# Cached attention of the sample tokens: from one stage after the attention groups to one step inside each of the four groups

## The reference, cut to what matters

```
def cached_attention(q, k_new, v_new, k_past, v_past, sinks, table):
    k_all = jnp.concatenate([k_past, k_new], axis=1)
    v_all = jnp.concatenate([v_past, v_new], axis=1)
    ...
    valid = (dist >= 0) & (dist < WINDOW)
    return sink_attend(q, k_all, v_all, dist, valid[None, None], sinks, table)

y = o.reshape(B, T, ATT_WIDTH) * jax.nn.silu(gate)
return x + rmsnorm(y @ w_out, g_post)
```

## Time and profile before

| | us |
|---|---|
| median of the runs shown | 3196.15 (3192.51 to 3197.89) |
| the profiled execution | 3192.12 |
| its span, first to last instruction | 3190.2 |
| PE busy | 2826.0 (89%) |
| DVE, ACT, POOL busy | 1177.4, 712.4, 1342.1 |
| mean granted TensorE clock | 0.941 |

### The profile page before, as it was taken

The page is one execution under the profiler, slowest core; times in us unless marked ns, Lnnn a source line. Parts: engine busy times, 40 slices in busy tenths (PEclk is TensorE's granted clock), DMA queues, the critical chain, the costliest instruction groups (busy, mean ns, idle before and its releaser), DMA issues.

```text
span 3190.2 us, 50357 instructions
## 1 busy us (share of the span) xinstructions
PE 2826.0 (89%) x17686; PEld 2725.6 (85%) x17686; DVE 1177.4 (37%) x2805; ACT 712.4 (22%) x1671; POOL 1342.1 (42%) x2013
## 2 busy tenths in 40 slices
PE   3999999999979999589999999999999802699994
PEld 3999999999979999488899889988988802699993
DVE  8344355433550000655541553455155401100006
ACT  4023212221140101223221322233133201110103
POOL 1244354443533333774556455554645400133323
PEclk7999999999989999899999999999999955799996
DMA  8221121211132222721111111111211111322227
GB/s 247 81 67 59 43 63 59 63 43 59 56 133 73 66 75 67 293 92 38 51 47 52 47 44 58 46 44 41 65 38 50 42 52 43 124 69 70 73 101 244
DMA packets 302784, 245.38 MB, mean 77 GB/s; under 512 B 11978, under 2 KB 279466, under 8 KB 301515
## 3 DMA queue, kind: packets, MB, share of 16 engines
q1 hardware_dynamic: 250684, 180.38, 17.9%
q10 hardware_dynamic: 51944, 63.03, 5.7%
HBM read 184.54 MB, written 63.15 MB: 78 GB/s over the span
## 4 chain that ended last, share of the span: by engine, by line
PE 81%; DVE 8%; SPq 6%; issue 2%; ACT 1%; DMA 1%; DVEq 0%; POOL 0%; ACTq 0%; POOLq 0%
PE ps L498 71%; SPq L355 6%; PE ps L535 3%; PE ps L590 2%; PE ps L616 2%; PE ps L603 2%; DVE xsp L1042 1%; DVE xsp L1244 1%; ACT pt L926 1%; DVE xsp L1107 1%; DVE xsp L1038 1%; DVE rstd L1215 1%; DMA vc<-out_sample_v 0%; PE ps L637 0%; PE ps L706 0%
## 5 line engine op out<-in xcount | busy, mean ns | idle before, releaser
L498 PE MATMUL ps<-xsp,wsp 128*128 128x344 f32 x14976 | 2422.9, 322 | 86.8 <-DVE mx L1264 24.3
L498 PEld LDWEIGHTS ps<-xsp,wsp 128*128 128x128 f32 x14976 | 2367.2, 189 | 130.4 <-issue 63.4
L397 POOL CAST wsp<-raw 128x512 fp32r<-128x512 f32 x272 | 219.1, 806 | 1178.9 <-PE ps L498 1048.1
L402 POOL TENSOR_SCALAR raw<-raw,prm 128x128 f32<-128x128 f32 x640 | 242.5, 396 | 475.7 <-PE ps L498 475.7
L399 POOL TENSOR_TENSOR wsp<-raw,wsp 128x512 fp32r<-128x512 f32 x272 | 400.0, 1470 | 50.4 <-POOL wsp L397 50.4
L1202 DVE TENSOR_TENSOR acc<-acc,stg 128x1032 f32<-128x1032 f32 x32 | 39.5, 1236 | 666.7 <-ACT stg L848 666.7
L409 POOL TENSOR_TENSOR wsp<-raw,wsp 128x512 fp32r<-128x512 f32 x160 | 220.5, 1378 | 29.4 <-POOL wsp L406 29.4
L406 POOL TENSOR_SCALAR wsp<-raw 128x128 fp32r<-128x128 f32 x640 | 184.1, 314 | 32.4 <-POOL raw L402 32.4
L847 ACT ACTIVATE stg<-ps 128x344 f32<-128x344 f32 x96 | 45.4, 473 | 641.3 <-PE ps L498 641.3
L913 ACT ACTIVATE mx<-mx 128x2 f32<-128x2 f32 x128 | 26.3, 206 | 442.6 <-DVE mx L1270 442.6
L916 ACT ACTIVATE pp<-pp,mx 128x256 f32<-128x256 f32 (+1 forms) x256 | 123.5, 484 | 0.0
(11 more groups left out here) (193 smaller groups left out, 2064.0 us busy)
## 6 DMA issues: line engine op xcount, KB each, us to landing
raw<-in_a_w_in SPq DMA_DIRECT2D x128, 256.0 KB, 2.8
raw<-in_b_w_qg SPq DMA_DIRECT2D x128, 256.0 KB, 2.8
o_t<-stg ACTq DMA_DIRECT2D x32, 516.0 KB, 3.6
xsp<-o_t SPq DMA_DIRECT2D x8, 2064.0 KB, 12.9
raw<-in_a_w_out SPq DMA_DIRECT2D x64, 256.0 KB, 2.7
raw<-in_b_w_out SPq DMA_DIRECT2D x64, 256.0 KB, 2.7
xsp<-x_t SPq DMA_DIRECT2D x7, 2064.0 KB, 17.1
x_t<-stg ACTq DMA_DIRECT2D x16, 516.0 KB, 2.8
```

The source lines that it names most:

```text
L397: pool.tensor_copy(hi, w).then_inc(S["w_hi"], 1)
L402: op = pool.tensor_scalar(w[:, k], w[:, k], prm[:, k0 + k, gain:gain + 1], 1.0, ALU.mult, ALU.mult)
L498: op = pe.matmul(ps[:, b0 + g, 0:TG], wsp[:, slots[j], wh, k, :], xsp[:, kk, xh, grp(g)], start=(j == 0 and k == 0 and n == 0), stop=(j == ...
```

## The change

The sample stage is taken out. Each of the four groups handles the cached attention of its own pair of key/value heads, for all 8 sequences. K of that pair comes as one transfer of 128 rows by 8 sequences by 128 numbers (512 KB) from ACT's queue into the space of `k1`, as soon as the last scores have been read; then one small transfer puts the new rows over partition 0. PE transposes K at position 75, scores follow at 77, the transposition of the probabilities at 79, the value product after chunk 9. V takes the same space once K is transposed. The scores are now one 64 by 128 tile: one row for each sequence and head. SP loads the bias for it (`sbias`) twice per group from `bias_row`, and the sinks (`nsks`) at the start by four small DMAs; the reordering of the tables at the start goes. `pt` has one buffer where it had two.

The restaging of `y` for O2 moves into the last group (written out behind the loop): quarters in order 0 to 3, with the last two `y` tiles taken from `q` without a trip to DRAM.

```
+        def sample_keys(i):
+
+            act.wait_ge(S["s_read"], i * 32 + 33)
+            act.dma_start(kcv, ck[:, :, bass.ds(i * P, P)]).then_inc(S["smp_k_in"], 16)
+
+        def sample_new_key(i):
+
+            act.wait_ge(S["smp_k_in"], i * 32 + 16)
+            act.wait_ge(S["kv_out"], i * 64 + 128)
+            act.dma_start(kcv[0:1, :, :], skn[:, :, bass.ds(i * P, P)]).then_inc(S["smp_k_in"], 16)
...
+        def sample_new_value(i):
+
+            act.wait_ge(S["smp_v_in"], i * 32 + 16)
+            act.dma_start(kcv[0:1, :, :], svn[:, :, bass.ds(i * P, P)]).then_inc(S["smp_v_in"], 16)
...
+            todo += [(72, 0, lambda: sample_keys(i)), (73, 1, lambda: sample_new_key(i)), (75, 1, lambda: sample_turned(i)),
+                     (77, 0.5, lambda: sample_new_value(i)), (77, 1, lambda: sample_exp(i)), (79, 1, lambda: sample_probs(i))]
...
+                for kq, at in enumerate((79.5, 81, 83)):
+                    todo.append((at, 4, lambda kq=kq: restage(64, SEQ, (kq,))))
+                todo.append((85, 4, lambda: restage(64, SEQ, (3,), 2)))
+                todo.append((85, 5, lambda: last_tiles(i)))
```

More of the change, by code:

```diff
@@ L332, in group @@
                         .then_inc(S[f"b_in{j % 2}"], 16)
+                if c == 5:
+                    if not first:
+                        sp.wait_ge(S["smp_dve"], i * 3 - 2)
+                    for r0, n, j0 in ((1, P - 1, BLK), (0, 1, 2 * BLK - 1)):
+                        sp.dma_start(sbias[:, r0:r0 + n], bias_row[bass.ds(i * NB, NB), j0:j0 + n]
+                                     .rearrange("(o h) n -> o h n", o=1).to_broadcast([NB, NB, n]), allow_slow_non_contiguous=True).then_inc(S["smp_b_in"], 16)
                 if first and c == 0:
@@ L552, in _, with out_phase @@
             a_block(i)
-        def out_phase(c_base, w_base, ready, order):
+        def out_phase(c_base, w_base, ready):
             for m in range(2):
-                gemm(m + c_base, m * NQ + w_base, m, ready, order=range(NQ) if m else order)
+                gemm(m + c_base, m * NQ + w_base, m, ready)
             with pe.Fori(1, O_ITERS) as i:
@@ L1355, in _ @@
+            if last:
+                todo.append((78.5, 5, lambda: sample_gate(slice(0, 12), own)))
+                for kq, at in enumerate((79.5, 82, 83)):
+                    todo.append((at, 6, lambda kq=kq: y_stage(kq, own)))
+                todo.append((82, 5.5, lambda: sample_gate(slice(12, 16), own)))
+                todo.append((85, 6, lambda: y_stage(3, own)))
             for _, _, f in sorted(todo, key=lambda x: x[:2]):
                 f()
-        own = Chain(dve, S["dve_step"], own.end(B_ITERS))
@@ L1386, in _ @@
-        own.link(dve.tensor_scalar(sx[:, 1, :], sx[:, 0, :], -1.0, None, ALU.mult))
-        dve.tensor_tensor(sx[:, 2, :], sx[:, 5, :], sx[:, 1, :], ALU.add).then_inc(S["smp_dve"], 1)
-        dve.wait_ge(S["smp_act"], 9)
-        own.link(dve.tensor_tensor(sx[:, 5, :], sx[:, 3, :], sx[:, 4, :], ALU.add))
-        own.link(dve.reciprocal(sx[:, 5, :], sx[:, 5, :]))
-        for n in range(2):
-            op = dve.tensor_scalar(sbm[:, n, :], sbm[:, n, :], sx[:, 5, n:n + 1], None, ALU.mult)
-        op.then_inc(S["smp_dve"], 1)
@@ new lines, in y_stage @@
+        def y_stage(kq, own):
+            k4 = slice(kq * QK, kq * QK + QK)
+            dve.wait_ge(S["stage_hi"], 32 + kq * QK + 1)
+            own.link(dve.tensor_copy(xsp[:, k4, 0, SEQ:NT], qs[:, k4, 0, :]))
+            own.step(dve.tensor_tensor(xsp[:, k4, 1, SEQ:NT], qs[:, k4, 0, :], xsp[:, k4, 0, SEQ:NT].bitcast(F32), ALU.subtract))
+            for n in range(QK):
+                k = kq * QK + n
+                y = land[:, k, 1, 0:SEQ] if k < KT - 2 else q[:, k % 2, 0:SEQ]
+                dve.wait_ge(S["stage_hi"], 32 + k + 1)
+                dve.tensor_tensor(xsp[:, k, 1, 0:SEQ], y, xsp[:, k, 0, 0:SEQ].bitcast(F32), ALU.subtract).then_inc(S["stage_used"], 1)
@@ L1411, in _ @@
+        B_STEPS = 4 + 32 * 3 + 4
+        with dve.Fori(0, B_ITERS - 1) as i:
+            own = Chain(dve, S["dve_step"], base, B_STEPS, i)
+            attention(i, own, False)
+            own.end()
+        own = Chain(dve, S["dve_step"], base + B_STEPS * (B_ITERS - 1))
+        attention(B_ITERS - 1, own, True)
         clear_acc()
-        restage(40, SEQ, (3, 0))
         out_phase(C_O2, 1)
```

304 lines of the change are left out of this document (129 added, 175 removed).

## The result

The changed kernel takes **3034.17 us** (median of 4 executions, 3032.7 to 3035.9), the kernel before 3194.33 (median of 4, 3189.3 to 3197.9): a ratio of 0.950, 95% interval 0.9483 to 0.9516. It is 160 us faster. The forecast was 3020, its range 3008 to 3045. In the profiled executions the spans are 3190.2 and 3034.0 us, so 156.2 us went where 176.2 were forecast.

The account below looks back on a forecast made before the run. The prediction took TensorE's instruction list plus a 204.2 us gap before O2 as the bound. Groups +15.8, tail -191.7 and start -0.3 took 3192.1 to 3015.9; the median's 4.0 made it 3020, range 3008 to 3045.

Parts of the forecast that it names:

- a rival's band: In the tail into O2, VectorE's staging sets the pace of quarters 1 to 3: 3028 to 3045 us, chance 26%.

## What to carry to other kernels

Before a stage is hidden under other work, ask why it is slow: here the number of rows of a transfer was worth 142 us by itself, and the hiding 18. When a sum comes out right, check that it is right for its reasons: a range that holds the result through a rival's band has not confirmed the forecast. When short steps are put on a path that another engine's long instructions share, cost them with one such instruction each; cutting those instructions in four took most of the loss away at no price that TensorE felt. Count only the catches that the path feels: twelve of the 20 here cost nothing. And when an edit of nothing costs 11 us, look for small operations that last as long as a neighbour's large one, before calling it noise.

## What the runs showed of the hardware

- A VectorE operation of 128x2 that starts 0.005 to 0.021 us behind GpSimd's 1.3 us subtraction takes 1.3 us and ends with it; started ahead of it, it takes 0.16. On the path of TensorE one such catch cost 0.8 us (0.4 in two of the chunks), off it nothing. Between two versions that differ by one moved DMA issue this was 11 us.
- TensorE's wait at the loop's branch was 2.35 and 1.94 us behind short matmuls, 0.73 and 1.07 behind a gemm, and none with the groups written out. The clock stood at 0.50 for 4 us behind the first; a quarter at the lower clock also came behind short matmuls without a branch.
- One row of eight 512-byte runs holds ACT's queue for 0.64 to 0.79 us as a load, and for 0.30 as a store.
